# Where eight transposes per step stand among TensorE's products, in a two-layer trunk with an expert stage

## The reference, cut to what matters

```
def swiglu(x, wg, wu, wd):
    return (jax.nn.silu(x @ wg) * (x @ wu)) @ wd

def moe_swiglu(x, w_router, we_gate, we_up, we_down):
    logits = (x @ w_router).astype(jnp.float32)
    top_vals, top_idx = lax.top_k(logits, TOP_K)
    gates = jax.nn.softmax(top_vals, axis=-1)
    combine = jnp.einsum("bske,bsk->bse", jax.nn.one_hot(top_idx, N_EXPERTS, dtype=jnp.float32), gates)
    out = jnp.zeros_like(x)
    for e in range(N_EXPERTS):
        out = out + combine[..., e:e + 1] * swiglu(x, we_gate[e], we_up[e], we_down[e])
    return out

for i in range(DEPTH):
    mix = hybrid_mixer(...)
    x = layer_norm(ALPHA * x + mix, ln1_g[i], ln1_b[i])
    ffn = swiglu(...) if i % 2 == 0 else moe_swiglu(...)
    x = layer_norm(ALPHA * x + ffn, ln2_g[i], ln2_b[i])
```

## Time and profile before

| | |
|---|---|
| median of 3 runs | 1344.29 us (1343.87 to 1344.55) |
| the profiled execution | 1344.4 us, its span 1342.7 us |
| PE busy | 1327.6 us (99%), 6623 matmuls and transposes |
| DVE busy | 1118.2 us (83%) |
| ACT busy | 914.1 us (68%) |
| share of the granted TensorE clock over the span | 0.997 |
| read from memory | 428.92 MB, 324 GB/s over the span |

### The profile page before, as it was taken

The page is one execution under the profiler, slowest core; times in us unless marked ns, Lnnn a source line. Parts: engine busy times, 40 slices in busy tenths (PEclk is TensorE's granted clock), DMA queues, the critical chain, the costliest instruction groups (busy, mean ns, idle before and its releaser), DMA issues.

```text
span 1342.7 us, 15943 instructions
## 1 busy us (share of the span) xinstructions
PE 1327.6 (99%) x6623; PEld 1121.2 (84%) x6623; DVE 1118.2 (83%) x827; ACT 914.1 (68%) x676; POOL 42.5 (3%) x56
## 2 busy tenths in 40 slices
PE   9999999999999999999999999999999999999996
PEld 9988888889888888888888888888888888888885
DVE  5877555587799998888889898888988989888996
ACT  5565444444787777777777777777777777777774
POOL 0100000010000000000000000000000000001100
PEclk9999999999999999999999999999999999999998
DMA  9938665556469999999999999999999999999992
GB/s 322 353 111 277 192 189 188 188 164 205 165 239 394 384 374 385 389 384 381 386 355 373 396 387 376 376 396 360 368 398 386 381 377 392 372 363 384 394 396 84
DMA packets 204386, 435.80 MB, mean 325 GB/s; under 512 B 8164, under 2 KB 50196, under 8 KB 204308
## 3 DMA queue, kind: packets, MB, share of 16 engines
q1 hardware_dynamic: 200464, 421.06, 86.4%
q0 software_dynamic: 3760, 13.63, 2.9%
q10 hardware_dynamic: 84, 0.02, 0.0%
HBM read 428.92 MB, written 5.77 MB: 324 GB/s over the span
## 4 chain that ended last, share of the span: by engine, by line
PE 97%; DVE 3%; issue 0%; ACT 0%; POOL 0%; DVEq 0%; POOLq 0%
PE turn L1369 17%; PE turn L1371 17%; PE turn L1370 17%; PE accp L1369 10%; PE accp L1371 10%; PE accp L1370 10%; PE turn L1481 3%; PE turn L1478 3%; PE accp L1688 2%; PE turn L1480 1%; PE turn L1479 1%; PE turn L1385 1%; PE accp L1411 0%; PE accp L1780 0%; DVE small L873 0%
## 5 line engine op out<-in xcount | busy, mean ns | idle before, releaser
L825 DVE TENSOR_TENSOR w_lo<-raw,w_hi 128x2048 fp32r<-128x2048 f32 (+1 forms) x401 | 906.4, 2269 | 138.2 <-ACT w_hi L525 134.8
L525 ACT CAST w_hi<-raw 128x2048 fp32r<-128x2048 f32 x395 | 755.5, 1916 | 226.2 <-PE turn L1371 108.6
L1369 PE MATMUL turn<-w_hi,a_hi 128*128 128x512 f32 x888 | 351.0, 395 | 0.4 <-DVE w_lo L825 0.4
L1371 PE MATMUL turn<-w_hi,a_lo 128*128 128x512 f32 x888 | 346.5, 390 | 0.0
L1370 PE MATMUL turn<-w_lo,a_hi 128*128 128x512 f32 x888 | 345.8, 389 | 0.0
L1371 PEld LDWEIGHTS turn<-w_hi,a_lo 128*128 128x128 f32 x888 | 166.7, 188 | 35.5
L1369 PEld LDWEIGHTS turn<-w_hi,a_hi 128*128 128x128 f32 x888 | 166.8, 188 | 33.7 <-DVE w_lo L825 0.8
L1370 PEld LDWEIGHTS turn<-w_lo,a_hi 128*128 128x128 f32 x888 | 166.9, 188 | 33.3
L1369 PE MATMUL accp<-w_hi,hT_hi 128*128 128x512 f32 x448 | 176.0, 393 | 0.0
L1371 PE MATMUL accp<-w_hi,hT_lo 128*128 128x512 f32 x448 | 174.5, 390 | 0.0
L1370 PE MATMUL accp<-w_lo,hT_hi 128*128 128x512 f32 x448 | 174.4, 389 | 0.0
(11 more groups left out here) (238 smaller groups left out, 1165.0 us busy)
## 6 DMA issues: line engine op xcount, KB each, us to landing
raw<-in_we_gate SPq DMA_DIRECT2D x112, 1024.0 KB, 7.7
raw<-in_we_up SPq DMA_DIRECT2D x112, 1024.0 KB, 8.1
raw<-in_we_down SPq DMA_DIRECT2D x112, 1024.0 KB, 7.6
raw<-in_w_in SPq DMA_DIRECT2D x18, 1024.0 KB, 8.7
raw<-in_w_down SPq DMA_DIRECT2D x11, 1024.0 KB, 5.2
raw<-in_w_gate SPq DMA_DIRECT2D x10, 1024.0 KB, 5.4
raw<-in_w_up SPq DMA_DIRECT2D x10, 1024.0 KB, 5.5
raw<-in_w_out SPq DMA_DIRECT2D x8, 1024.0 KB, 10.5
```

What stands on the lines that cost most here:

```text
L525: nc.scalar.copy(w_hi[:, p % PARTS, :], raw[:, p % RING, :]).then_inc(hi_done, 1)
L825: return nc.vector.tensor_tensor(out, whole, hi.bitcast(f32), ALU.subtract)
L1369: nc.tensor.matmul(to, lh, rh, start=start, stop=False, **group)
L1371: return nc.tensor.matmul(to, ll, rh, start=False, stop=stop, **group)
```

## The change

The four transposes of h no longer stand in a row between gate and up. Each is issued by itself: one ahead of each of the first four values of k of up, so that three matmuls of 512 columns lie between two transposes. The four transposes of the fetched token rows leave `after_up` and go the same way among the other four values of k of up. The waits go with the first transpose of four and the signal with the last. The transposes themselves, their operands and their results are the same.

```
-            def half_step(to, half, xg, w):
+            def half_step(to, half, xg, w, between=None):
...
                 for kk in range(KD // 2):
                     k = half * (KD // 2) + kk
+                    if between is not None:
+                        between(kk)
                     last = product(to, [a[:, k, :] for a in xg], (wh[:, kk, :], wl[:, kk, :]), k == 0, k == KD - 1)
...
-            def rows_step(i, which):
+            def rows_step(i, which, turned=(None, None)):
...
-                              split(step_at(i) + 2 * which + half)).then_inc(piece_used, 1)
+                              split(step_at(i) + 2 * which + half), turned[half]).then_inc(piece_used, 1)
+
+            def turn_h(i):
+
+                def block_of(b):
+                    if b == 0:
+                        pe.wait_ge(e_h, i + 1)
+                    last = transpose_block(h_e[:, i % 2, :], b)
+                    if b == COL // P - 1:
+                        last.then_inc(e_hT, 1)
+                return block_of
...
             def turn_tokens(e, half):
-                pe.wait_ge(tokens_loaded, 16 * (e - 1))
-                pe.wait_ge(tokens_known, e // 2)
-                if half_of(e, half):
-                    pe.wait_ge(xg_done, half_of(e, half))
-                for k in range(4):
+
+                def block_of(k):
+                    if k == 0:
+                        pe.wait_ge(tokens_loaded, 16 * (e - 1))
+                        pe.wait_ge(tokens_known, e // 2)
+                        if half_of(e, half):
+                            pe.wait_ge(xg_done, half_of(e, half))
                     cols = slice((4 * half + k) * P, (4 * half + k + 1) * P)
                     last = nc.tensor.transpose(misc_tokens[:, k, :], more_rows[:, cols], ident[:])
-                last.then_inc(xg_turned, 1)
+                    if k == 3:
+                        last.then_inc(xg_turned, 1)
+                return block_of
+
+            def turned_in(i):
+
+                at = tokens_at(*divmod(i, STEPS))
+                return (turn_h(i - 1) if i else None, turn_tokens(*at) if at is not None else None)
...
-                at = tokens_at(e, s)
-                if at is not None:
-                    turn_tokens(*at)
...
-                if 0 < i < N_STEPS:
-                    pe.wait_ge(e_h, i)
-                    transpose_h(h_e[:, (i - 1) % 2, :]).then_inc(e_hT, 1)
                 if i < N_STEPS:
-                    rows_step(i, 1)
+                    rows_step(i, 1, turned_in(i))
                     after_up(i)
```

More of the change, by code:

```diff
@@ L1683, in transpose_pick, with transpose_block @@
                 return last
+            def transpose_block(h, b):
+                return nc.tensor.transpose(accp[:, 2, b * P:(b + 1) * P], h[:, b * P:(b + 1) * P], ident[:])
             def transpose_h(h):
                 for b in range(COL // P):
-                    last = nc.tensor.transpose(accp[:, 2, b * P:(b + 1) * P], h[:, b * P:(b + 1) * P], ident[:])
+                    last = transpose_block(h, b)
                 return last
-            def half_step(to, half, xg, w):
+            def half_step(to, half, xg, w, between=None):
                 wh, wl = [a.rearrange("p (k f) -> p k f", k=KD // 2) for a in w]
```

## The result

The changed kernel takes 1348.78 us (median of 7 runs, 1348.32 to 1350.12), the one before 1344.41 in the same session (1343.83 to 1344.55). The ratio is 1.0033, with an interval of 1.0023 to 1.0042: slower, by 4.4 us. The profiled execution took 1349.96 us.

A forecast was written before the change was run, and what follows sets the result against it. TensorE was taken as the bound, busy 949.5 of 950 us in the expert stage. Terms 5.0 - 0.4 + 0.1 = 4.7 us on the profiled 1344.4 gave 1349.1 us, range 1343 to 1353.5.

The forecast's parts named there:

- 5.0 - 0.4 + 0.1 = 4.7: Whole kernel, us: returns to long matmuls 5.0 more, tails cut by token transposes 0.4 back, late VectorE 0.1 more.
- main case: Expert stage: each added return from transpose to long matmuls costs 0.015 to 0.035 us; 1347 to 1351.5 us, chance 0.50.
- A transpose's own price, difference 0: Moved transposes on TensorE: four cost 4 x 0.11 us in a row or singly, through uncovered weight loads.
- The second rival: Single transposes: two weight sets held ready hide the next load, under 0.10 us each; 1332.9 or 1337.6 us, chance 0.12.
- 201 breaks at 0.025: Expert stage: 201 more returns from a transpose to long matmuls, 0.025 us each, 5.0 us more.
- the first rival: Expert stage: single transposes don't disturb the matmuls behind, 0.79 us between transposes; 1344.0 to 1345 us, chance 0.30.
- "Nobody on TensorE waits", 0.1 us: Expert stage: later turned h still reaches TensorE in time; 0.1 us taken for VectorE in the last expert.
- The shift of `e_hT`: Signal after the fourth transpose of h: some 2.1 us later, delaying ACT's and DVE's work behind it.
- The margins of the two pieces and of `hT_lo`: DVE's results for down: `hT_lo` ready 2.1 us before TensorE wants it, the two pieces 1.3 and 1.7 us.
- bound of 1.9 us for VectorE in the last expert: Last expert's four steps with row additions: DVE 0.8 us over per step, 3.2 less 1.3 margin, at most 1.9 us.
- The third rival: Expert stage: VectorE becomes the bound, down waits for its second piece, 0.1 us in 55 steps; 1354.6 us, chance 0.08.
- Token rows, transfers, banks: Expert stage: earlier token rows, transfers with over 4 us of room, and PSUM bank changes each cost 0.

The follow-up runs named there:

- the last step in a row: The changed kernel, but in the last step alone the four transposes of h stand in a row ahead of up; 1347.59 us.
- twice the distance: Against the changed kernel: transposes of h singly with six 512-column matmuls between two, token rows in fours behind up; 1409.61 us.
- the second pair: Against the changed kernel: transposes of h two by two, three matmuls between the pairs, token rows in fours behind up; 1345.16 us.

## Why the prediction was right or wrong

**Right: the forecast and its sign.** 1349.1 us forecast, 1348.78 measured, inside the range. But two of its terms erred in opposite directions: 5.0 - 0.4 + 0.1 = 4.7 was the sum, and 2.6 + 1.5 + 0.15 = 4.3 is what the trace shows at equal clock. That the total came so close is luck: with the breaks as measured and nobody waiting, as the prediction had it, the time would have been 1347.0, at the lower edge of its main case.

- *A transpose's own price, difference 0: right.* 0.11 us singly, the load behind it uncovered as before. The second rival, which needed under 0.10, fell, and with it the reading of the Trainium skill's sentence by two sets of weights ("TensorE: Matmul & The Clock Gate", part 2, step 1); the trace agrees with one set ahead.
- *201 breaks at 0.025: mis-sized.* Measured 0.013 to 0.016 each, 2.6 us with the tokens, where the prediction had 5.0 - 0.4 = 4.6. From one single transpose to the next 0.815 was expected and 0.803 measured, about half way to the first rival's 0.79. The step that failed was to take the first three matmuls of the tail behind a row of four as those behind a single one; the mechanism held, since 0.007, 0.015 and up to 0.03 were measured for one, three and six matmuls between. The first rival, no change, had its point of decision at 0.013 and lost narrowly on this term alone: without the end the change would have been 2.6 us, at the edge of what can be told.
- *"Nobody on TensorE waits", 0.1 us: wrong.* The shift of `e_hT` was found, and its size too: ACT waits 1.92 us for it. The margins of the two pieces and of `hT_lo` held in the change. What was left out was the third reader: h itself, in the one step where its transposes stand in down. 1.5 us. The prediction's bound of 1.9 us for VectorE in the last expert was of another kind (the row additions, and the pieces as what comes late); with the last step in a row, where DVE only came late from the steps before, the wait was 0.3. Setting the last four aside as "not touched" hid that the instructions that feed them were moved.
- *The third rival* was given 0.1 us in 55 steps and a chance of 0.08. In the change it did not happen in the steps. At twice the distance it did, with ten times its price.
- *Token rows, transfers, banks: right at 0.* No new line of waits of TensorE names them.

## What to carry to other kernels

In this kernel, spreading short TensorE instructions among long ones hid only their own weight load; the load behind each was uncovered just the same, so four in a row and four singly cost alike (0.11 us each), and the row has fewer returns and signals earlier. Before a producer is stretched, write down for each reader when it is next wanted, in the last round of the loop as well as in the middle: here a delay of 2 us cost nothing in 54 rounds and 1.5 us in the last, and one of 4 us cost about 1 us in every round. A right total can hide two wrong terms, so check the terms in the trace.

## What the runs showed of the hardware

- Behind short instructions, the next matmuls of 512 columns are some ns late each, up to 0.05 us over ten, and less when the next short one comes sooner: 0.007, 0.015 and up to 0.03 us behind a transpose with one, three and six of them between. Its cause was not found, nor why the tail's length differs (2.32 us for ten behind a row of four, 2.30 behind the second pair, 2.27 undisturbed).
- The granted clock fell to half (1.2 GHz) for about 3 us in the router in two of the ten profiled executions, behind waits and products of 8 columns, and cost 1.3 us there; in the other eight it stayed at 1.00 behind the same work. The levels 1.1 to 1.4 us apart in the runs go with the clock granted over the whole span (0.997, 0.996, 0.994). Where in the span the unprofiled runs lost it is not known, and no experiment was made on it.
